# The scores of a pair of heads move from the next step into the middle of the same step's weight unit

## The chip, the cores and the metric

The kernel runs on one core of a Trainium2 chip. The metric is the time of one execution on the device in microseconds (us). Before the change it is 1480.53 us, the median of three runs (1478.89 to 1480.69).

## What is computed

Two blocks of two transformer layers each, on 256 rows of width 1024, in float32. The change touches the attention of the first block's two layers. There, eight index heads score all keys; their sum picks the 64 keys that the six heads of kind A may see. Five heads of kind B (a band with a relative bias) and five of kind C (a forgetting mask) have masks of their own. Cut to what matters:

```python
# index heads: 8 of width 64, with one common key
idx_scores = einsum('bqhs,bqh->bqs', relu(einsum('bqhd,bsd->bqhs', qis, kf)), ws)
_, sel = top_k(where(adm, idx_scores, -inf), topk)
# heads A, B, C: 16 of width 64, each with its own mask or bias
logits = einsum('bqhd,bshd->bhqs', q, k) * scale + mask
p = softmax(logits)
o = einsum('bhqs,bshd->bqhd', p, v)
# beside them, from the same normed rows h: the gates of the three branches
gates = sigmoid(h @ w_gate + b_gate)
y = (gates[0] * (o_a @ w_a) + gates[1] * (o_b @ w_b) + gates[2] * (o_c @ w_c)) @ w_out
```

## The kernel before

The 256 rows are two tiles of 128. A weight matrix comes in units of two tiles of 128 rows by 512 columns. ScalarE rounds a unit to a high part (`hi_units`, L1294), GpSimd makes the low part (`lo_units`, L730), and TensorE multiplies high by high, high by low and low by high: 12 matmuls of 512 columns a unit (L776), the first six with the unit's first tile, the last six with its second. `unit` takes a function `amid` and calls it between these two sixes.

The attention of a layer of the first block is 27 steps, k = 0 to 26, written out engine by engine in the function `attention`. The 24 heads come in pairs: four pairs of index heads (heads 0 to 7), then eight pairs of real heads (8 to 23). In its step k TensorE does in this order:

- the scores of the pair k - 1 where k is odd (`pipe["score"]` is 1): L1006 and L1009. A score contracts over 64 values, so the two heads of a pair use the upper and the lower half of the array's rows; the profile shows such matmuls as 64*128. They wait for `qk_turned` (ScalarE's copy of the turned queries and keys), for `masked` of the head before the pair (its scores have left the two banks that all pairs share, 4 and 5), and for pair 0 also for `drained` of a modulation product that used such a bank;
- the turning (transposes, L1022) of the queries and keys of the pair k, where k is even;
- the turning of the probabilities of head k - 3 (L986, `turn_head`);
- through `weave`: in steps 3 to 8 the products for a forgetting mask (L1181 to L1188), then a weight unit of the gates (steps 0 to 23) or of a branch (24 to 26). In its middle stand, where k is even and from 12 on, the products of the pair k - 4, k - 3 with V (L966, L968, `weigh_pair`). Each head takes 64 of the array's columns: 128*64 in the profile.

ScalarE in its step k rounds a weight unit, copies the turned queries and keys of the pair k (L1420 to L1425), and only then takes head k - 1: a ReLU in its bank for an index head (L1433), the exponentials for a real one (L1437, L1439). VectorE in its step k makes a forgetting mask from TensorE's products of that step (L2054, L2055, steps 4 to 8), and then takes head k - 1: for an index head it adds the bank to the sum of scores (L1870), for a real head it adds the mask (L1880, L1881); both set `masked`. Then it copies the turned probabilities of head k - 3 (L1849), on which the products with V wait, and after that come gate rows, the low part of a pair's output and a round of the search for the 64 best keys. Within an engine this order is fixed by the code. The attention of the second block (`paired` false) keeps its order.

Of the kernel before, what the change touches and what calls it, by code (L numbers as in the profile page):

```python
# [329 lines left out]
def heads_one():  # L330

    out = [dict(kind="I", h=h, q=QI + h * DH, k=KI) for h in range(HI)]
    out += [dict(kind="B", h=h, q=QB + h * DH, k=KB + h * DH, v=VB + h * DH, o=(HA + h) * DH) for h in range(HB)]
    out += [dict(kind="C", h=h, q=QC + h * DH, k=KC + h * DH, v=VC + h * DH, o=(HA + HB + h) * DH) for h in range(HC)]
    out += [dict(kind="A", h=h, q=QA + h * DH, k=KA + h * DH, v=VA + h * DH, o=h * DH) for h in range(HA)]
    return out
# [13 lines left out]
def program(nc, ctx, dram, out, cat, book):  # L350
# [101 lines left out]
    def con(name):  # L452
        a, b = cat[name]
        return CON[:, a:b]
# [30 lines left out]
    def tp_user_before(pipe, h):  # L485

        return max((g for g in range(h) if pipe["tp"][g] == pipe["tp"][h]), default=-1)

    def score_bank(pipe, h):
        return BANK[pipe["sb"][h // 2 % len(pipe["sb"])][h % 2]]  # L490
# [246 lines left out]
    def _(pe):  # L737
# [203 lines left out]
        def attention(tag, heads, src, weave, pipe, after=None):  # L941


            real = lambda h: 0 <= h < len(heads) and heads[h]["kind"] != "I"

            def weigh_head(h):
                if real(h):
                    bank = BANK[pipe["tp"][h]]
                    copied = p_turned_act if pipe["act_copies"] and h % 2 else p_turned
                    pe.wait_ge(copied.sem, copied.at((tag, h)))  # L950
                    v = heads[h]["v"]
                    pt = pipe["pt"][:, h % pipe["n_pt"], :]
                    pe.matmul(bank[:, 384:448], pt[:, 0:P], src[:, 0, v:v + DH], start=True, stop=True)  # L953
                    pe.matmul(bank[:, 448:512], pt[:, P:2 * P], src[:, 0, v:v + DH], start=True, stop=False)
                    pe.matmul(bank[:, 448:512], pt[:, 2 * P:3 * P], src[:, 1, v:v + DH], start=False, stop=True)\
                        .then_inc(headed.sem, headed.mark((tag, h)))

            def weigh_pair(h):

                if real(h) and h % 2:  # L960
                    bank = BANK[pipe["tp"][h - 1]]
                    pe.wait_ge(p_turned.sem, p_turned.at((tag, h)))
                    values = [heads[h - 1 + n]["v"] for n in range(2)]
                    turned_probs = [pipe["pt"][:, (h - 1 + n) % pipe["n_pt"], :] for n in range(2)]
                    for n in range(2):
                        pe.matmul(bank[n * DH:(n + 1) * DH, 0:S], src[:, 0, values[n]:values[n] + DH], turned_probs[n][:, 0:S], start=True, stop=False)  # L966
                    for n in range(2):
                        ins = pe.matmul(bank[n * DH:(n + 1) * DH, P:S], src[:, 1, values[n]:values[n] + DH], turned_probs[n][:, S:S + P], start=False, stop=True)  # L968
                    ins.then_inc(headed.sem, headed.mark((tag, h)))

            def turn_head(h):
                if real(h):
                    if pipe["paired"]:
                        pe.wait_ge(evened.sem, evened.at((tag, h)))
                        if h % 2 and pipe["tp"][h - 1] == pipe["tp"][h]:
                            pe.wait_ge(p_turned.sem, p_turned.at((tag, h - 1)))
                        elif real(h - 2) and pipe["tp"][h - 2] == pipe["tp"][h]:
                            pe.wait_ge(turned_lo.sem, turned_lo.at((("o", tag), (h - HI) // 2 - 1)))
                    else:
                        pe.wait_ge(exped.sem, exped.at((tag, h)))  # L980
                    if not pipe["paired"] and real(tp_user_before(pipe, h)):

                        pe.wait_ge(head_out.sem, head_out.at((tag, tp_user_before(pipe, h))))
                    bank = BANK[pipe["tp"][h]]
                    for at, cols in ((0, slice(S, S + P)), (P, slice(0, P)), (2 * P, slice(P, S))):
                        ins = pe.transpose(bank[:, at:at + P], SM[:, h % N_SM, cols], con("ident"))  # L986
                    ins.then_inc(p_in_psum.sem, p_in_psum.mark((tag, h)))

            for k in range(len(heads) + pipe["weigh"]):
                h = k - pipe["score"]  # L990
                if 0 <= h < len(heads) and h % 2 == 0:
                    pe.wait_ge(qk_turned.sem, qk_turned.at((tag, h // 2)))
                    last = h + 1 - 2 * len(pipe["sb"])
                    if last >= 0:

                        pe.wait_ge(masked.sem, masked.at((tag, last)))
                    if h == 2 and heads[0]["kind"] != "I":

                        pe.wait_ge(drained.sem, drained.at(("qkv", tag[1], -(-3 * len(heads) * DH // CW) - 1)))
                    if h == 0 and heads[0]["kind"] == "I":  # L1000
                        pe.wait_ge(drained.sem, drained.at(("ada", tag, (7, 9)[tag])))
                    slot = h // 2 % pipe["n_qk"]
                    kk = KIT[:, :] if heads[h]["kind"] == "I" else pipe["qk"][:, slot, S:2 * S]
                    for n in range(2):
                        rows_ = slice(n * DH, (n + 1) * DH)
                        pe.matmul(score_bank(pipe, h + n)[:, 0:S], pipe["qk"][rows_, slot, P:S], kk[rows_, :], start=True, stop=True)  # L1006
                    for n in range(2):
                        rows_ = slice(n * DH, (n + 1) * DH)
                        pe.matmul(score_bank(pipe, h + n)[:, S:S + P], pipe["qk"][rows_, slot, 0:P], kk[rows_, 0:P], start=True, stop=True)\  # L1009
                            .then_inc(scored.sem, scored.mark((tag, h + n)))  # L1010
                if k < len(heads) and k % 2 == 0:
                    one, two = heads[k], heads[k + 1]
                    assert one["kind"] == "I" or two["k"] - one["k"] == two["q"] - one["q"] == DH
                    if k >= 2:
                        pe.wait_ge(qk_turned.sem, qk_turned.at((tag, k // 2 - 1)))
                    with_k = one["kind"] != "I" or one["h"] == 0
                    if one["kind"] == "I" and one["h"] == 0:
                        pe.wait_ge(act_side.sem, act_side.at(("keys", tag)))
                    for what, at in (("q", 0), ("k", S))[:2 if with_k else 1]:
                        for t in range(NT):  # L1020
                            cols = KEY2[:, t, :] if one[what] == two[what] else src[:, t, one[what]:one[what] + 2 * DH]
                            ins = pe.transpose(BANK[TQ][:, at + t * P:at + (t + 1) * P], cols, con("ident"))  # L1022
                    ins.then_inc(qk_in_psum.sem, qk_in_psum.mark((tag, k // 2)))
                if pipe["paired"]:
                    turn_head(k - pipe["turn"])
                    weave(k, lambda: weigh_pair(k - pipe["weigh"]))
                else:
                    weigh_head(k - pipe["weigh"])
                    weave(k)
                    turn_head(k - pipe["turn"])  # L1030
                    if after is not None:
                        after(k)
# [95 lines left out]
        for l in range(DEPTH):  # L1128
# [29 lines left out]
            heads = heads_one()  # L1158

            def weave(k, amid, l=l):  # L1160
                if 3 <= k < 3 + HC + 1:
                    forget_products(l, k - 3)
                if k < 4 * N_GATE:
                    unit(by_key["gate", l, k // 4], k % 4, HT, amid=amid)
                else:
                    c, u = (((0, "C"), 0), ((0, "C"), 1), ((1, "C"), 0))[k - 4 * N_GATE]
                    branch_unit(l, *c, u)
                    amid()

            def branch_unit(l, cc, b, u):  # L1170

                pe.wait_ge(turned_lo.sem, turned_lo.at((("o", l), {"C": (3, 4), "B": (1, 2), "A": (N_PAIRS - 2, N_PAIRS - 1)}[b][u])))
                unit(by_key["branch", l, cc, b], u, HT if b == "A" else BT)
# [46 lines left out]
        for i in range(2):  # L1220
            heads = heads_two(i)
# [1187 lines left out]
```

## Time and profile before

| what | value |
|---|---|
| median of three runs | 1480.53 us |
| the profiled execution | 1479.98 us, its span 1478.2 us |
| TensorE busy with matmuls | 1450.4 us (98%) |
| TensorE busy with weight loads | 1214.7 us (82%) |
| VectorE, ScalarE, GpSimd busy | 720.7, 744.9, 1203.2 us |
| attention steps of layer 0 | about 121.0 to 231.0 us |
| attention steps of layer 1 | about 550.2 to 660.2 us |

The span is the time from the first to the last instruction that the profile holds; the execution is 1.8 us longer. In a timeline a row gives start, duration, engine, line, operation and tiles, and how many instructions of one kind it joins; the start plus the duration is its end. Matmuls overlap, so that a row can start before the one ahead of it has ended. In the chain of waits, the pieces lie end to end: there the cost of a group of matmuls is read directly. A float32 matmul of the scores, of V and of the transposes stands there as two records, so that L1006 x4 are two instructions.

### The profile page before, as it was taken

The page shows a single profiled execution, that of the slowest core. Times are in us where ns is not written, and L with a number is a line of the kernel's source. Part 1 is how long each engine was busy: PE and PEld are TensorE (multiplying, and loading weights), DVE is VectorE, ACT ScalarE, POOL GpSimd, SP SyncE. Part 2 cuts the span into 40 slices and gives each one's busy share as a digit, 9 for nine tenths or more (in the row PEclk, how much of TensorE's full clock was granted, in tenths as well). Part 3 has the DMA queues.
Part 4 walks back from the last instruction along what each step waited for, and adds up shares of the span by engine and source line. Part 5 has one row for each costly group of instructions (what it writes and reads, how often), then busy time and mean ns, then how long its engine had stood idle before and what let it go on. Part 6 is the DMA issues. An engine that isn't in the chain of part 4 may idle for free.

```text
span 1478.2 us, 21666 instructions
## 1 busy us (share of the span) xinstructions
PE 1450.4 (98%) x7666; PEld 1214.7 (82%) x7666; DVE 720.7 (49%) x1575; ACT 744.9 (50%) x1242; POOL 1203.2 (81%) x978
## 2 busy tenths in 40 slices
PE   7999999999999999999999999999999999999997
PEld 4898777799988988777888888778888887788886
DVE  7663664766643754745566214364650044655202
ACT  3335674644444435765544445465654345555441
POOL 4799988888878977558998989908999978489994
PEclk9999999999999999999999999999999999999999
DMA  9995547688875986337775566704555757156561
GB/s 357 387 349 177 174 161 233 223 312 312 309 264 176 394 296 215 114 98 238 236 241 186 192 199 172 239 29 157 188 193 196 221 155 226 62 163 202 192 199 57
DMA packets 149685, 313.87 MB, mean 212 GB/s; under 512 B 10933, under 2 KB 31817, under 8 KB 149577
## 3 DMA queue, kind: packets, MB, share of 16 engines
q1 hardware_dynamic: 147824, 311.15, 62.9%
q10 hardware_dynamic: 1754, 1.35, 0.3%
q8 instruction: 61, 1.00, 0.3%
q14 instruction: 46, 0.38, 0.1%
HBM read 311.39 MB, written 1.06 MB: 211 GB/s over the span
## 4 chain that ended last, share of the span: by engine, by line
PE 93%; DVE 3%; ACT 2%; POOL 1%; issue 1%; DMA 0%; SPq 0%; DVEq 0%; ACTq 0%
PE bank L776 58%; PE bank L821 12%; PE bank L822 8%; PE bank L819 5%; PE bank L1006 1%; PE bank L986 1%; PE bank L1022 1%; POOL lo_units L730 1%; PE bank L857 1%; PE bank L966 1%; DVE bank L1668 1%; ACT hi_units L1294 1%; PE bank L953 1%; PE bank L1009 1%; PE bank L1107 0%
## 5 line engine op out<-in xcount | busy, mean ns | idle before, releaser
L730 POOL TENSOR_TENSOR lo_units<-raw_units,hi_units 128x512 fp32r<-128x512 f32 (+3 forms) x928 | 1150.6, 1276 | 233.1 <-ACT hi_units L1294 232.2
L1294 ACT ACTIVATE hi_units<-raw_units 128x1024 fp32r<-128x1024 f32 (+1 forms) x470 | 483.3, 1031 | 434.4 <-PE bank L776 271.1
L776 PE MATMUL bank<-hi_units,turned 128*128 128x512 f32 (+3 forms) x1600 | 438.3, 388 | 1.5 <-DVE turned L1716 0.8
L776 PEld LDWEIGHTS bank<-hi_units,turned 128*128 128x128 f32 x1600 | 292.7, 188 | 52.7 <-issue 3.1
L822 PE MATMUL bank<-turned,lo_units 128*128 128x256 f32 x1024 | 288.2, 281 | 0.0
L776 PE MATMUL bank<-hi_units,turned_wide 128*128 128x512 f32 x992 | 274.5, 391 | 0.0
L821 PE MATMUL bank<-turned,hi_units 128*128 128x512 f32 x736 | 260.6, 399 | 0.0
L776 PE MATMUL bank<-lo_units,turned 128*128 128x512 f32 (+3 forms) x800 | 252.6, 383 | 0.8 <-POOL lo_units L730 0.5
L776 PEld LDWEIGHTS bank<-hi_units,turned_wide 128*128 128x128 f32 x992 | 185.3, 188 | 38.5 <-issue 0.5
L822 PEld LDWEIGHTS bank<-turned,lo_units 128*128 128x128 f32 x1024 | 194.3, 190 | 0.2
L776 PEld LDWEIGHTS bank<-lo_units,turned 128*128 128x128 f32 x800 | 149.8, 188 | 29.9 <-POOL lo_units L730 3.2
L821 PEld LDWEIGHTS bank<-turned,hi_units 128*128 128x128 f32 x736 | 138.3, 188 | 34.3
L776 PE MATMUL bank<-lo_units,turned_wide 128*128 128x512 f32 x496 | 160.6, 389 | 0.0
L1668 DVE SCALAR_TENSOR_TENSOR bank<-ada_units,small,bank 128x512 f32<-128x512 f32 x144 | 108.8, 756 | 36.1 <-DMA ada_units<-in_ada_w 31.5
L776 PEld LDWEIGHTS bank<-lo_units,turned_wide 128*128 128x128 f32 x496 | 93.1, 188 | 19.6
L1734 DVE TENSOR_REDUCE bank<-bank 128x256 f32<-128x512 f32 x92 | 64.3, 699 | 86.5 <-PE bank L822 85.6
L819 PE MATMUL bank<-turned,hi_units 128*128 128x256 f32 x576 | 104.0, 283 | 0.0
L819 PEld LDWEIGHTS bank<-turned,hi_units 128*128 128x128 f32 x576 | 90.2, 192 | 0.6
L1601 ACT ACTIVATE mlp_relu<-bank 128x256 f32<-128x256 f32 x56 | 21.6, 385 | 60.6 <-DVE bank L1734 60.1
L2183 DVE SCALAR_TENSOR_TENSOR bank<-x_rows,bank 128x512 f32<-128x512 f32 x8 | 5.2, 693 | 89.5 <-PE bank L776 89.5
L1730 DVE TENSOR_TENSOR turned_wide<-bank,turned_wide 128x256 fp32r<-128x256 f32 x92 | 39.0, 424 | 13.8 <-ACT turned_wide L1328 11.1
L2196 DVE SCALAR_TENSOR_TENSOR bank<-x_rows,bank 128x512 f32<-128x512 f32 x8 | 5.6, 696 | 75.4 <-PE bank L776 75.2
(264 smaller groups left out, 1325.6 us busy)
## 6 DMA issues: line engine op xcount, KB each, us to landing
ada_units<-in_ada_w SPq DMA_DIRECT2D x88, 512.0 KB, 7.8
raw_units<-in_w_ffn_tiles SPq DMA_DIRECT2D x72, 512.0 KB, 5.3
raw_units<-in_mlp_w_out SPq DMA_DIRECT2D x64, 512.0 KB, 3.3
raw_units<-in_mlp_w_tiles SPq DMA_DIRECT2D x56, 512.0 KB, 3.3
raw_units<-in_w_in SPq DMA_DIRECT2D x56, 458.0 KB, 9.8
raw_units<-in_w_in SPq DMA_DIRECT2D x48, 512.0 KB, 6.6
raw_units<-in_w_ffn_out SPq DMA_DIRECT2D x44, 512.0 KB, 3.8
raw_units<-in_moba_w_qkv SPq DMA_DIRECT2D x24, 512.0 KB, 3.8
```

Source lines behind the costliest of these rows:

```text
L730: pool.tensor_tensor(LO[:, s, b, 0:w], RAW[:, u["slot"], b, 0:w], HI_[:, s, b, 0:w].bitcast(F32), ALU.subtract).then_inc(lo_ready.sem, lo_ ...
L776: ins = pe.matmul(BANK[2 * c["pair"] + t][:, 0:w], (A[a] if A is BT else A[:, a])[:, part, t * P:(t + 1) * P], W[:, s, b, 0:w], start=(i = ...
L819: pe.matmul(bank[:, 0:S], HI_[:, s, b, at:at + P], A[:, kt, part, :], start=kt == 0 and part == 0, stop=False)
L821: pe.matmul(bank[:, :], HI_[:, s, b, at:at + P], A[:, kt, :, :].rearrange("p two s -> p (two s)"), start=kt == 0, stop=False)
L822: ins = pe.matmul(bank[:, 0:S], LO[:, s, b, at:at + P], A[:, kt, 0, :], start=False, stop=kt == KT - 1)
L857: ins = pe.transpose(BANK[(TQ, TP)[n % 2]][:, j * P:(j + 1) * P], src[:, t, (4 * half + j) * P:(4 * half + j + 1) * P], con("ident"))
L953: pe.matmul(bank[:, 384:448], pt[:, 0:P], src[:, 0, v:v + DH], start=True, stop=True)
L1294: act.activation(HI_[:, s, 0:n, 0:w], RAW[:, u["slot"], 0:n, 0:w], ACT.Copy)\
L1601: act.activation(RTN[:, m % 4, :], BANK[(TQ, TP)[m % 2]][:, 0:S], ACT.Relu).then_inc(act_side.sem, act_side.mark(("relu tile", i, m)))
L1668: ins = v.scalar_tensor_tensor(total, raw[:, k, :], COND[:, kt:kt + 1], partial, ALU.mult, ALU.add)
L1730: tell(v.tensor_tensor(AT[:, n, 1, :], h, AT[:, n, 0, :].bitcast(F32), ALU.subtract), turned_lo, (tag, "tile", n))
L1734: return v.tensor_reduce(to, bank[:, :].rearrange("p (two s) -> p s two", two=2), AX_X, ALU.add)
```

## The change

The scores become a function, `score_pair`. In the first block's layers it is no longer called at the start of step k + 1, but in the middle of step k's unit, right behind `weigh_pair`, and for the pair k that was turned at the start of this same step. The second block calls it where it stood.

```diff
-            for k in range(len(heads) + pipe["weigh"]):
-                h = k - pipe["score"]
+            def score_pair(h):
+
                 if 0 <= h < len(heads) and h % 2 == 0:
                     pe.wait_ge(qk_turned.sem, qk_turned.at((tag, h // 2)))
...
+            for k in range(len(heads) + pipe["weigh"]):
+                if not pipe["paired"]:
+                    score_pair(k - pipe["score"])
                 if k < len(heads) and k % 2 == 0:
...
                 if pipe["paired"]:
                     turn_head(k - pipe["turn"])
-                    weave(k, lambda: weigh_pair(k - pipe["weigh"]))
+
+                    def tiled(k=k):
+                        weigh_pair(k - pipe["weigh"])
+                        score_pair(k)
+
+                    weave(k, tiled)
```

No instruction is added or removed on any engine; only TensorE's order changes. Its order in steps 2 and 3 of layer 0, the pair of index heads 2 and 3 (L1022 turns its queries, L776 is the gate unit, L1006 and L1009 are its scores), before:

```order
L1022 MATMUL bank<-constants,proj_rows 128x128 [waits qk_turned]
L1022 MATMUL bank<-constants,proj_rows 128x128
L776 MATMUL bank<-hi_units,turned 128x512 [waits hi_ready]
L776 MATMUL bank<-hi_units,turned 128x512 x3
L776 MATMUL bank<-lo_units,turned 128x512 [waits lo_ready]
L776 MATMUL bank<-lo_units,turned 128x512
L776 MATMUL bank<-hi_units,turned 128x512 x4
L776 MATMUL bank<-lo_units,turned 128x512 [waits lo_ready]
L776 MATMUL bank<-lo_units,turned 128x512
L1006 MATMUL bank<-idx_keys_turned,qk_turned 128x256 [waits masked,qk_turned]
L1006 MATMUL bank<-idx_keys_turned,qk_turned 128x256
L1009 MATMUL bank<-idx_keys_turned,qk_turned 128x128 x2
```

The same place on TensorE in the changed kernel, where the turning is L1026:

```order
L1026 MATMUL bank<-constants,proj_rows 128x128 [waits qk_turned]
L1026 MATMUL bank<-constants,proj_rows 128x128
L776 MATMUL bank<-hi_units,turned 128x512 [waits hi_ready]
L776 MATMUL bank<-hi_units,turned 128x512 x3
L776 MATMUL bank<-lo_units,turned 128x512 [waits lo_ready]
L776 MATMUL bank<-lo_units,turned 128x512
L1006 MATMUL bank<-idx_keys_turned,qk_turned 128x256 [waits masked,qk_turned]
L1006 MATMUL bank<-idx_keys_turned,qk_turned 128x256
L1009 MATMUL bank<-idx_keys_turned,qk_turned 128x128 x2
L776 MATMUL bank<-hi_units,turned 128x512 x4
L776 MATMUL bank<-lo_units,turned 128x512 [waits lo_ready]
L776 MATMUL bank<-lo_units,turned 128x512
```

The scores with their two waits have moved ahead of the unit's last six matmuls; between the turning and the scores six matmuls are left of twelve.

TensorE's order in steps 12 and 13 of layer 0, from the products of heads 8 and 9 with V (L966, L968) to the turned probabilities of head 10 (L986), before:

```order
L966 MATMUL bank<-probs_turned,proj_rows 64x256 [waits p_turned]
L966 MATMUL bank<-probs_turned,proj_rows 64x256
L968 MATMUL bank<-probs_turned,proj_rows 64x128 x2
L776 MATMUL bank<-hi_units,turned 128x512 x4
L776 MATMUL bank<-lo_units,turned 128x512 [waits lo_ready]
L776 MATMUL bank<-lo_units,turned 128x512
L1006 MATMUL bank<-qk_turned 128x256 [waits masked,qk_turned]
L1006 MATMUL bank<-qk_turned 128x256
L1009 MATMUL bank<-qk_turned 128x128 x2
L986 MATMUL bank<-constants,scores 128x128 [waits turned_lo,evened]
```

The same place on TensorE in the changed kernel:

```order
L966 MATMUL bank<-probs_turned,proj_rows 64x256 [waits p_turned]
L966 MATMUL bank<-probs_turned,proj_rows 64x256
L968 MATMUL bank<-probs_turned,proj_rows 64x128 x2
L1006 MATMUL bank<-qk_turned 128x256 [waits masked,qk_turned]
L1006 MATMUL bank<-qk_turned 128x256
L1009 MATMUL bank<-qk_turned 128x128 x2
L776 MATMUL bank<-hi_units,turned 128x512 x4
L776 MATMUL bank<-lo_units,turned 128x512 [waits lo_ready]
L776 MATMUL bank<-lo_units,turned 128x512
L986 MATMUL bank<-constants,scores 128x128 [waits turned_lo,evened]
```

The products with V and the scores now stand side by side, and the six full matmuls that parted them come behind both.

## Rows read from the trace of the kernel before

**Rows 1.** The page, its first part: busy time, share and instructions of each engine.

```profile
PE 1450.4 (98%) x7666; PEld 1214.7 (82%) x7666; DVE 720.7 (49%) x1575; ACT 744.9 (50%) x1242; POOL 1203.2 (81%) x978
```

**Rows 2.** Chain of waits, layer 0, steps 8 to 14: start, duration (us), what.

```profile
157.56 2.97 PE bank L776 x12
...
168.60 1.39 PE bank L776 x6
169.99 0.58 PE bank L966 x4
170.57 0.22 PE bank L968 x4
170.79 1.58 PE bank L776 x6
172.37 0.63 PE bank L1006 x4
173.00 0.22 PE bank L1009 x4
173.22 0.48 PE bank L986 x3
...
176.90 0.33 PE bank L986 x3
```

**Rows 3.** Timeline of TensorE, layer 0: halves of the units of steps 0, 2, 4.

```profile
122.38 0.62 PE L776 MATMUL bank<-lo_units,turned 128*128 128x512 f32 x2
...
129.18 0.62 PE L776 MATMUL bank<-lo_units,turned 128*128 128x512 f32 x2
...
136.16 0.59 PE L1188 MATMUL bank<-constants,small 128*128 128x256 f32 x2
...
137.51 0.62 PE L776 MATMUL bank<-lo_units,turned 128*128 128x512 f32 x2
```

**Rows 4.** Timeline of ScalarE, layer 0, steps 0 and 2.

```profile
122.03 0.38 ACT L1422 ACTIVATE qk_turned<-bank 128x256 f32<-128x256 f32 x1
...
128.45 0.38 ACT L1422 ACTIVATE qk_turned<-bank 128x256 f32<-128x256 f32 x1 [0.25 <-PE bank L1022]
128.74 0.49 ACT L1433 ACTIVATE bank<-bank 128x384 f32<-128x384 f32 x1
```

**Rows 5.** Timeline of VectorE, layer 0, steps 0, 2 and 4.

```profile
122.17 0.69 DVE L1689 TENSOR_TENSOR mod_rows<-bank,row_vectors 128x512 f32<-128x512 f32 x1
...
129.35 0.74 DVE L1870 SCALAR_TENSOR_TENSOR idx_scores<-bank,proj_rows,idx_scores 128x256 f32<-128x256 f32 x2 [1.62 <-ACT bank L1433]
...
136.86 0.48 DVE L2054 SCALAR_TENSOR_TENSOR forget_masks<-bank,small,constants 128x256 f32<-128x256 f32 x1 [3.03 <-PE bank L1188]
...
137.64 0.74 DVE L1870 SCALAR_TENSOR_TENSOR idx_scores<-bank,proj_rows,idx_scores 128x256 f32<-128x256 f32 x2
```

**Rows 6.** Timeline of TensorE, layer 1, step 0: end of the unit's first half.

```profile
551.60 0.62 PE L776 MATMUL bank<-lo_units,turned 128*128 128x512 f32 x2
```

**Rows 7.** Timeline of ScalarE, layer 1, step 0.

```profile
551.88 1.06 ACT L1294 ACTIVATE hi_units<-raw_units 128x1024 fp32r<-128x1024 f32 x1 [0.29 <-DMA raw_units<-in_w_in]
...
553.11 0.38 ACT L1422 ACTIVATE qk_turned<-bank 128x256 f32<-128x256 f32 x1
```

**Rows 8.** Timeline of VectorE, layer 1, step 0.

```profile
552.13 0.69 DVE L1693 SCALAR_TENSOR_TENSOR mod_rows<-bank,row_vectors 128x512 f32<-128x512 f32 x1
```

**Rows 9.** Chain of waits, layer 0, step 16.

```profile
186.90 0.57 DVE probs_turned L1849
...
187.51 0.65 PE bank L966 x4
```

**Rows 10.** Timeline of TensorE, layer 0: the first halves of steps 16 and 18.

```profile
186.62 0.62 PE L776 MATMUL bank<-lo_units,turned 128*128 128x512 f32 x2
...
195.58 0.61 PE L776 MATMUL bank<-lo_units,turned 128*128 128x512 f32 x2
```

**Rows 11.** Timeline of VectorE, layer 0, step 18: the copy before the products with V.

```profile
195.42 0.56 DVE L1849 COPY probs_turned<-bank 128x384 f32<-128x384 f32 x1
```

## The prediction, made before the changed kernel was run

> **What bounds the kernel now.** I read the page first. TensorE is busy with matmuls for 1450.4 of 1478.2 us, 98%; VectorE and ScalarE stand at half of the span [rows 1]. Busy time at 98% says that TensorE rarely waits for data. It doesn't say that it works at its peak, since matmul records cover the time in which the array fills and empties. So a change of order can bring something only where the array pauses inside "busy" time, and can cost something wherever TensorE begins to wait. Next I read the chain of waits through the attention of layer 0, where the pieces lie end to end, and after that the timelines of three engines around the places to which the scores move. Layer 1 repeats layer 0 to a few hundredths, save its step 0.
>
> **What a change of the array's tiling costs now.** The chain shows four such changes for a pair of real heads. Six full matmuls of a unit, in mid-stream, take 1.39 us. L968 and L1009 are four records of 128 columns in 0.22 us; L966 and L1006 have twice the columns, so they should take 0.44 and take 0.58 and 0.63. Going from full matmuls into the products with V costs 0.58 - 0.44 = 0.14, and into the scores 0.63 - 0.44 = 0.19. Coming out: the six behind L968 take 1.58, so 0.19; the transposes behind L1009 take 0.48 where the same three behind other full matmuls take 0.33, so 0.15 [rows 2]. Twelve matmuls behind scores take 2.97, that is 2 x 1.39 + 0.19: out of the scores into a unit costs 0.19 [rows 2]. The four together: 0.14 + 0.19 + 0.19 + 0.15 = 0.67 us per pair.
>
> **What the change saves.** In steps 12, 14, 16, 18, 20 and 22 (six pairs per layer) the products with V and the scores become neighbours. What is left is 0.14 in, x between the two, 0.19 out into the unit: 0.33 + x. No row shows x, since these two never meet before. From below x is 0: both are half-array shapes, and from L966 to L968, which share a shape, nothing is paid [rows 2]. From above it is a full way out and in, 0.19 + 0.19 = 0.38. I take x = 0.19, one ordinary change, since 64*128 and 128*64 cut the array in different directions and L1006 paid 0.19 wherever it followed another shape; that is the nearest row. The saving is then 0.67 - 0.52 = 0.15 us per pair; with x = 0 it is 0.34, with x = 0.38 it is -0.04.
>
> The Trainium skill, TensorEngine Tiling (Array Packing), section Tiling Modes, Key Properties, says that changing the tiling mode drains the TensorE, while a move between tiles of one mode does not. By that rule x is not 0, since the two are separate modes in its list; by the view that only full against half counts, x would be 0. The trace agrees with the rule where it can (0.14 to 0.19 us at each change, none from L966 to L968), but has no change between the two half shapes.
>
> Two of the six can't give all of this, because TensorE is not alone at the limit there. At step 16 the first half of the unit ends at 186.62 + 0.62 = 187.24 [rows 10], VectorE's copy of the turned probabilities at 186.90 + 0.57 = 187.47, and TensorE goes on at 187.51, with L966 at 0.65 instead of 0.58 [rows 2, 9]. This gives a price for any such wait: end of what it waits for, plus 0.04 + 0.07 = 0.11, minus the end of the matmuls before. TensorE already loses 0.34 there, and if it comes earlier it waits longer: the saving of step 14 is gone. At step 18 the copy ends at 195.42 + 0.56 = 195.98, and with 0.11 at 196.09; the matmuls end at 195.58 + 0.61 = 196.19 [rows 10, 11]: room for 0.10 of the saving of step 16. Per layer: 4 x 0.15 + 0 + 0.10 = 0.70 us, for two layers 1.4 us. (x = 0: 4 x 0.34 + 0.10, twice, 2.9 us. x = 0.38: 12 x -0.04, -0.5 us.)
>
> The six other pairs (steps 0 to 10) have no products with V beside them: one way in and one way out before, the same after. I cost that at 0.
>
> **What the change adds: waits in the index heads.** The scores keep their waits, but lose as cover the six matmuls of the unit's second half (1.39 us). For the pairs 2, 4, 6 and 8 they wait until the second head of the pair before has left the bank. For pair 2 the way there is ScalarE's copy of the queries (128.45 to 128.83, it waited for L1022), then the ReLU of head 1 behind it on ScalarE, from 128.74 [rows 4], then VectorE's sum, 129.35 + 0.74 = 130.09 [rows 5]. The first half of TensorE's unit ends at 129.18 + 0.62 = 129.80 [rows 3]. Price: 130.09 + 0.11 - 129.80 = 0.40 us. That head 1 is scored earlier doesn't help: its ReLU stands behind the copy of this step's queries, and that copy needs this step's turning. For pair 4 the sum of head 3 stands on VectorE behind the forgetting mask (136.86), which waits for L1188 of the same step (136.16 + 0.59 = 136.75), and ends at 137.64 + 0.74 = 138.38 [rows 3, 5]; the half unit ends at 137.51 + 0.62 = 138.13 [rows 3]. Price: 0.36. Pairs 6 and 8 repeat this pattern, 0.36 each. Both ways start from work of TensorE in the same step, so a later TensorE doesn't shorten them. Behind the waiting scores stand the last six matmuls and everything after them; nothing later in these steps has slack to give back. Sum per layer: 0.40 + 3 x 0.36 = 1.48 us.
>
> Pair 0. In layer 0 the queries are copied by 122.03 + 0.38 = 122.41 [rows 4], and the modulation product has left its bank by 122.17 + 0.69 = 122.86 [rows 5]; with 0.11 that is 122.97, and the half unit ends at 122.38 + 0.62 = 123.00 [rows 3]: nothing. In layer 1 the half unit ends at 551.60 + 0.62 = 552.22 [rows 6], but ScalarE is behind a weight unit that waited for its DMA until 551.88, and copies the queries only at 553.11 + 0.38 = 553.49 [rows 7]. Price: 553.49 + 0.11 - 552.22 = 1.38 us. If the DMA were early, VectorE's modulation rows, 552.13 + 0.69 = 552.82 [rows 8], would still ask 0.71. I take 1.38, as the trace has it.
>
> From pair 8's successors on the wait for `masked` is free: in steps 12 to 22 VectorE does the mask before the copy for which the products with V wait anyway. ScalarE's and VectorE's own orders don't move, GpSimd and the DMA queues get no new work, and the second block is untouched: 0 for each.
>
> **Sum.** Waits 2 x 1.48 + 1.38 = 4.3 us; saving 1.4 us; net +2.9 us. The profiled execution would go from 1479.98 (span 1478.2 and 1.8 around it) to 1482.9. The median of the runs lies 0.55 above it, so I predict 1480.53 + 2.9 = 1483.4 us, slower by 0.2%. That is about what a measurement of this kernel can tell from no change (0.2%, 2.96 us), so the sign of the verdict hangs on tenths of a microsecond.
>
> **Rivals.**
> - *The two half shapes follow each other free* (x = 0). For: the two heads of a pair run beside each other without a pause in either shape. Against: every change of shape in the chain cost something. Time: waits 4.3, saving 2.9: +1.4, 1481.9 us. Chance 0.25.
> - *Clearly slower.* At the place where V and scores meet the array empties and loads in turn, x = 0.38: saving -0.5, net +4.8, 1485.3 us. For: weight loads can't be hidden across a change, and here two changes touch. Against: L966 is entered for 0.14 although it loads two halves. It decides from x = 0.20 on, where the net passes 2.96 us (4.3 - 8 x (0.34 - x) - 0.2). Chance 0.18.
> - *The index waits don't arise*, because the earlier scores pull ReLU and sum ahead in ScalarE and VectorE. For: both engines idle in these steps (1.62 us before the sum of head 1 [rows 5]). Against: the order described above. Then only pair 0 of layer 1 costs: 1.38 - 1.4, about 0, 1480.5 us; with x = 0 as well, -1.5, 1479.0 us; if that pair's DMA is early too, under 1478. Chance 0.12.
> - The forecast itself, 1483.4: 0.45.
>
> **How the numbers follow.** The forecast's own spread (the pair 0 wait from 0.7 to 1.4, x within 0.1) puts it between 1482.0 and 1484.5: of its 0.45 I put 0.26 within 0.2% and 0.19 beyond. The free change is within (0.23) or just beyond (0.02). The dear change is slower (0.17; 0.01 within). No index waits: within 0.07, faster 0.05. Faster 0.05, same 0.57, slower 0.38. Range: 1480.4, which takes in the free change and the edge of no index waits, to 1485.6, which takes in the dear change.
>
> **What would show it.** In the profile after: TensorE idle before L1006 on VectorE's L1870 (pairs 2 to 8) of 0.3 to 0.4 us, eight times, and once of about 1.3 us on ScalarE's copy in layer 1; in the chain, L966, L968, L1006, L1009 in a row, with L1006 at 0.63 for x = 0.19, 0.44 for x = 0; the step pair from one L966 to the next shorter by 0.15 except around steps 14 to 18, with the wait before L966 at step 16 growing from 0.27 to about 0.4. Wrong would be: no idle before L1006 (then the second engine orders gave way), or idle before L966 in other steps (then VectorE bounds more of the stage than I read).

## The result, and the profile after

The changed kernel takes 1483.72 us, median of 10 runs (1481.84 to 1487.38), beside 1480.08 us for the kernel before (10 runs). The ratio is 1.0023, 95% interval 1.0015 to 1.0031: slower by 2.2 to 4.6 us. The forecast was 1483.4 us, 2.9 us slower.

Who waited for whom on TensorE in the changed kernel: us in total, times, longest. These are the rows of the attention that are new or have grown:

```profile
PE bank L1006 <- DVE idx_scores L1879: 3.2, 8, 0.4
...
PE bank L966 <- DVE probs_turned L1858: 0.8, 2, 0.4
PE bank L1006 <- DVE mod_rows L1702: 0.7, 1, 0.7
```

L1006 are the scores, and L1879 is what was L1870 before (VectorE adds an index head to the sum). There are eight waits in two layers, four per layer, before the pairs 2, 4, 6 and 8. The third row is pair 0 of layer 1. L966 (products with V) waited before as well, once per layer at step 16 [rows 9]; the idle time is now 0.42 us each instead of 0.27.

The chain of waits of the changed kernel in step 2 of layer 0, where before there was no step off TensorE at all:

```profile
128.07 0.23 PE bank L1026 x2
...
128.60 0.50 ACT bank L1442
...
129.22 0.75 DVE idx_scores L1879 x2
129.97 0.14 issue
130.11 0.70 PE bank L1006 x4
130.81 0.22 PE bank L1009 x4
131.03 1.59 PE bank L776 x6
```

The way is the one of [rows 4, 5]: turning, ScalarE's ReLU behind the copy, VectorE's sum, scores. The first half of the unit had ended at 129.67 (in the timeline 129.05 + 0.62), so that without a wait L1006 would have ended at 129.67 + 0.63 = 130.30. It ends at 130.81: 0.51 us are lost. The same reckoning gives 0.45, 0.47 and 0.45 for pairs 4, 6 and 8; together 1.88 us per layer.

The chain of the changed kernel in steps 12 and 13 of layer 0, which answers to [rows 2]:

```profile
170.49 1.39 PE bank L776 x6
171.88 0.58 PE bank L966 x4
172.46 0.22 PE bank L968 x4
172.68 0.63 PE bank L1006 x4
173.31 0.22 PE bank L1009 x4
173.53 1.58 PE bank L776 x6
175.11 0.33 PE bank L986 x3
```

V and scores now stand side by side, and L1006 still takes 0.63 us: going from one half shape to the other costs 0.19, as much as coming from full matmuls. The transposes L986 have fallen from 0.48 to 0.33. From the first L966 to the next (180.37 in the same chain) it is 8.49 us; before, it was 8.61.

At step 16 of layer 0 the changed kernel waits as before, [rows 9] again:

```profile
188.67 0.57 DVE probs_turned L1858
189.24 0.04 issue
189.28 0.65 PE bank L966 x4
```

Pair 0 of layer 1 in the changed kernel, TensorE, ScalarE and VectorE, beside [rows 6 to 8]:

```profile
552.85 0.62 PE L776 MATMUL bank<-lo_units,turned 128*128 128x512 f32 x2
554.22 0.70 PE L1006 MATMUL bank<-idx_keys_turned,qk_turned 64*128 64x256 f32 x4 [0.75 <-DVE mod_rows L1702]
```

```profile
552.82 0.37 ACT L1431 ACTIVATE qk_turned<-bank 128x256 f32<-128x256 f32 x1
```

```profile
553.39 0.69 DVE L1702 SCALAR_TENSOR_TENSOR mod_rows<-bank,row_vectors 128x512 f32<-128x512 f32 x1
```

Relative to TensorE's turning, the last weight unit that ScalarE rounds before the copy, and that waits for its DMA, started 1.5 us earlier here than in the profile of before (at 551.59, with the turning at 551.48; before at 551.88, with the turning at 550.23). So its copy is done at 553.19, and VectorE's modulation rows, done at 554.09 in the chain, decide. Lost: 554.92 - (552.85 + 0.62 + 0.63) = 0.82 us.

The sum, per layer, from the turning of pair 0 to the last L966: layer 0 121.00 to 229.18 before, 120.82 to 230.50 now, +1.50 us; layer 1 550.23 to 658.39 before, 551.48 to 661.93 now, +2.29. Together 3.8 us, in the interval of the runs.

The profiled execution itself is only 2.2 us slower (1482.19 against 1479.98), since a stage whose instructions the change doesn't touch was faster in it. In the first MLP of the second block, matmuls of L821 and L822 follow each other in turns. In the ten profiles the time from one fixed turning before that stage (L857, 1021.05 in the profile of before) to the first behind it (1192.68) is either 171.6 us (the kernel before, three experiments, and a second profile of the changed kernel) or 170.3 (the first profile of the changed kernel and four experiments). The two profiles of the changed kernel alone differ by 1.38 us there. Whether the change has a hand in it is open: the four profiles in which this turning came before 1022 us all have 171.6, and of the six in which it came at 1023.8 or later five have 170.3 and one, the second of the changed kernel (1026.70), has 171.6. If the later start made the stage faster, the change would get back up to 1.4 of the 3.8 us, and that too would lie in the interval of the runs.

### The profile page after: what moved, and what is told of

Same layout as the page of the kernel before. It is cut to its first block, busy times and chain, and to the rows that moved or that the text cites. A ratio compares the mean times of both kernels' runs of the same rounds, so it can differ in the third digit from the quotient of the medians.

```text
span 1480.3 us, 21666 instructions
## 1 busy us (share of the span) xinstructions
PE 1448.0 (98%) x7666; PEld 1215.1 (82%) x7666; DVE 720.8 (49%) x1575; ACT 744.8 (50%) x1242; POOL 1203.1 (81%) x978
## 4 chain that ended last, share of the span: by engine, by line
PE 91%; DVE 4%; ACT 2%; issue 1%; POOL 1%; DMA 0%; SPq 0%; DVEq 0%; ACTq 0%
PE bank L776 57%; PE bank L821 12%; PE bank L822 8%; PE bank L819 5%; PE bank L1006 1%; PE bank L986 1%; PE bank L1026 1%; POOL lo_units L730 1%; PE bank L857 1%; PE bank L966 1%; DVE bank L1677 1%; ACT hi_units L1303 1%; PE bank L953 1%; PE bank L1009 0%; PE bank L1116 0%
## 5 line engine op out<-in xcount | busy, mean ns | idle before, releaser
L776 PE MATMUL bank<-hi_units,turned 128*128 128x512 f32 (+3 forms) x1600 | 439.6, 389 | 1.5 <-DVE turned L1725 0.8
L776 PEld LDWEIGHTS bank<-hi_units,turned 128*128 128x128 f32 x1600 | 292.0, 188 | 52.6 <-DVE turned L1782 1.2
L822 PE MATMUL bank<-turned,lo_units 128*128 128x256 f32 x1024 | 287.4, 281 | 0.0
L776 PE MATMUL bank<-hi_units,turned_wide 128*128 128x512 f32 x992 | 274.4, 391 | 0.0
L821 PE MATMUL bank<-turned,hi_units 128*128 128x512 f32 x736 | 259.2, 397 | 0.0
L776 PE MATMUL bank<-lo_units,turned 128*128 128x512 f32 (+3 forms) x800 | 252.7, 383 | 0.7 <-POOL lo_units L730 0.5
L776 PEld LDWEIGHTS bank<-hi_units,turned_wide 128*128 128x128 f32 x992 | 185.3, 188 | 38.4 <-issue 0.5
L822 PEld LDWEIGHTS bank<-turned,lo_units 128*128 128x128 f32 x1024 | 194.0, 189 | 0.2
L776 PEld LDWEIGHTS bank<-lo_units,turned 128*128 128x128 f32 x800 | 149.8, 188 | 30.1 <-POOL lo_units L730 3.2
L821 PEld LDWEIGHTS bank<-turned,hi_units 128*128 128x128 f32 x736 | 138.2, 188 | 33.6
L776 PE MATMUL bank<-lo_units,turned_wide 128*128 128x512 f32 x496 | 160.5, 389 | 0.0
L776 PEld LDWEIGHTS bank<-lo_units,turned_wide 128*128 128x128 f32 x496 | 93.1, 188 | 19.6
```

Source lines behind the costliest of these rows:

```text
L776: ins = pe.matmul(BANK[2 * c["pair"] + t][:, 0:w], (A[a] if A is BT else A[:, a])[:, part, t * P:(t + 1) * P], W[:, s, b, 0:w], start=(i = ...
L821: pe.matmul(bank[:, :], HI_[:, s, b, at:at + P], A[:, kt, :, :].rearrange("p two s -> p (two s)"), start=kt == 0, stop=False)
L822: ins = pe.matmul(bank[:, 0:S], LO[:, s, b, at:at + P], A[:, kt, 0, :], start=False, stop=kt == KT - 1)
```

## The experiments

My theory after the result: the early pairs (0 to 8) lose by waiting (1.88 us per layer, and pair 0 of layer 1), the late pairs (10 to 22) save by losing one change of shape (0.6 us per layer), and VectorE holds back part of that. The main rival: calling scores in the middle of a unit costs by itself.

### The late pairs alone

```diff
                 if not pipe["paired"]:
                     score_pair(k - pipe["score"])
+                elif (k - 1) <= HI:
+                    score_pair(k - 1)
...
                         weigh_pair(k - pipe["weigh"])
-                        score_pair(k)
+                        if not (k <= HI):
+                            score_pair(k)
```

> The change for the pairs 10 to 22 alone; the pairs 0 to 8 are scored at the start of the next step, as before. Theory (the loss is the early pairs' waits, the meeting of V and scores saves): no wait before L1006 on VectorE's index sums or on the modulation rows; L1006 right behind L968 at 0.63 us; about 0.53 us less per layer than before, 1.1 us in all, ratio 0.9993. Rival (scores in the middle of a unit cost by themselves, wherever they stand): as slow as the changed kernel or half-way, ratio 1.001 to 1.002.

Measured: 1479.66 us (11 runs) against 1479.53 for the kernel before (31 runs), ratio 1.0001 (0.9992 to 1.0009). The interval holds the expected 0.9993 and excludes the rival's 1.001 to 1.002. The profile decides more sharply: from the turning of pair 0 to the last L966 of layer 0 it is 107.66 us (before 108.18), 0.52 less, and among the waits L1006 has no row:

```profile
PE bank L986 <- ACT scores L1451: 1.8, 4, 0.7
...
PE bank L966 <- DVE probs_turned L1861: 0.8, 2, 0.4
```

So the middle of a unit costs next to nothing by itself: seven pairs per layer are scored there without a wait, and the layer is no slower. The saving stands in the trace, and is too small to tell from nothing in the times.

### The early pairs alone

The same edit with `> HI` and `not (k > HI)`.

> The change for the pairs 0 to 8 alone; the pairs 10 to 22 are scored at the start of the next step, as before. Theory: all the waits of the changed kernel and none of its saving: 2 x 1.96 us in the two layers, and 0.9 more at pair 0 of layer 1, +4.7 us on before, ratio 1.0032. Rival (the middle of a unit costs by itself): five of twelve pairs, so well under the changed kernel's ratio of 1.0023.

Measured: 1483.43 us (9 runs), ratio 1.0026 (1.0016 to 1.0036). Layer 0 takes 110.20 us from the same to the same point, +2.02. In layer 1, up to the last L966 but one, it is 104.72 against 101.95, +2.77. Together this is 4.8 us in the trace, 4.7 expected. The times show 3.9 us, with an interval of 2.4 to 5.3; this profile is one of those with the fast MLP stage. The rival is out: five of twelve pairs carry more than the whole loss.

```profile
PE bank L1006 <- DVE idx_scores L1882: 3.2, 8, 0.4
...
PE bank L1006 <- DVE mod_rows L1705: 0.7, 1, 0.7
PE bank L966 <- DVE probs_turned L1861: 0.5, 2, 0.3
```

### ScalarE and VectorE reordered

This starts from the changed kernel and touches the index head before each of the pairs 2, 4, 6 and 8. ScalarE does its ReLU ahead of the copies of the pair just turned:

```diff
                 weave(k)
+                h = k - pipe["score"]
+                early = k % 2 == 0 and 0 <= h < len(heads) and heads[h]["kind"] == "I"
+                if early:
+                    act.wait_ge(scored.sem, scored.at((tag, h)))
+                    score = score_bank(pipe, h)[:, 0:3 * P]
+                    act.activation(score, score, ACT.Relu).then_inc(exped.sem, exped.mark((tag, h)))
                 if k < len(heads) and k % 2 == 0:
...
-                if 0 <= h < len(heads) and heads[h]["kind"] == "I":
+                if early:
+                    pass
+                elif 0 <= h < len(heads) and heads[h]["kind"] == "I":
```

VectorE adds it to the sum ahead of what `weave` gives it in this step, such as the forgetting mask:

```diff
-                weave(k)
                 h = k - pipe["score"]
+                first_sum = k % 2 == 0 and 0 <= h < len(heads) and heads[h]["kind"] == "I"
+                if not first_sum:
+                    weave(k)
...
                         tell(ins, masked, (tag, h))
+                        if first_sum:
+                            weave(k)
```

> The changed kernel, and in steps 2, 4, 6 and 8 ScalarE does the ReLU of the head before the pair ahead of the copy of the pair's queries, and VectorE adds it to the sum ahead of the forgetting mask. Theory (the scores wait since these two stand behind work that needs TensorE's turning or forgetting products of the same step): the eight waits of 0.46 to 0.51 us are gone, the one at pair 0 of layer 1 stays; 3.8 us less than the changed kernel, -0.3 us on before, ratio 0.9998. Rival (ScalarE and VectorE get to head 1, 3, 5 or 7 too late in any order): the waits stay, ratio 1.0023.

Measured: 1479.71 us (11 runs), ratio 1.0001 (0.9992 to 1.0010); the expected 0.9998 lies in the interval. Step 2 of layer 0, VectorE and TensorE:

```profile
127.20 0.75 DVE L1889 SCALAR_TENSOR_TENSOR idx_scores<-bank,proj_rows,idx_scores 128x256 f32<-128x256 f32 x2 [1.77 <-ACT bank L1424]
```

```profile
127.90 0.38 PE L1026 MATMUL bank<-constants,proj_rows 128*128 128x128 f32 x2
...
129.04 0.63 PE L776 MATMUL bank<-lo_units,turned 128*128 128x512 f32 x2
129.60 0.70 PE L1006 MATMUL bank<-idx_keys_turned,qk_turned 64*128 64x256 f32 x4
```

The timeline gives L1006 0.70 us with or without a wait; the chain of this step shows that it now costs 0.63 and ends at 130.30, where it was reckoned above for no wait:

```profile
128.28 1.39 PE bank L776 x6
129.67 0.63 PE bank L1006 x4
130.30 0.22 PE bank L1009 x4
```

Head 1 is in the sum at 127.95, when TensorE has just begun to turn pair 2; in the changed kernel that was at 129.97, two microseconds later in the step. No wait on the index sums is left. So these two engines had the time; only their written order kept them. The two reorderings were made together, so this run doesn't tell their shares apart. The wait at pair 0 of layer 1 is still there (0.75 us), which is why the kernel is level with before and not ahead: layer 0 alone takes 0.34 us less than before.

### The late pairs alone, and VectorE's zeros moved

```diff
-                if k == HI + HB + ONE["score"] + 1:
+                if k == HI + HB + ONE["score"] + 4:
                     v.memset(BT[2][DH:P].bitcast(F32), 0.0)
                     link(v.memset(BT[3][0:DH].bitcast(F32), 0.0))
```

> As the kernel with the change for the pairs 10 to 22 alone, and VectorE's two clears of mixed_turned (L2073, L2074) moved from step 15 to step 18. Theory (VectorE bounds the steps 14 to 16, so that the saving of step 14 is lost there): the wait before L966 at step 16 goes, from one L966 to the next 8.49 us instead of 8.91; 0.45 us per layer less than the late pairs alone, about -2.0 us on before, ratio 0.9987. Rival (something else is late next there, ScalarE's evened probabilities or the mask): L966 waits as before, ratio 0.9993.

The edit of the late pairs alone stays in. Measured: 1477.41 us (11 runs) against 1479.53, ratio 0.9985 (0.9976 to 0.9994): the only kernel here that is clearly faster than the one before. From step 14 to 16 of layer 0, in the chain:

```profile
178.27 0.58 PE bank L966 x4
178.85 0.22 PE bank L968 x4
179.07 0.63 PE bank L1006 x4
...
184.61 0.44 PE bank L1028 x4
185.05 0.33 PE bank L986 x3
185.37 1.39 PE bank L776 x6
186.76 0.58 PE bank L966 x4
```

No VectorE stands in between, and it is 8.49 us from one L966 to the next, as expected. Layer 0 takes 107.17 us, 1.01 less than before. In layer 1 the profiled execution (1480.42 us, the slowest of the eleven) lost it again at pair 0, although that is scored at the old place:

```profile
550.66 0.38 PE L1028 MATMUL bank<-constants,idx_scores 128*128 128x128 f32 x2
555.06 0.70 PE L1006 MATMUL bank<-idx_keys_turned,qk_turned 64*128 64x256 f32 x4 [1.26 <-ACT qk_turned L1434]
```

The weights' DMA landed at 553.38, 2.7 us behind the start of this turning, and ScalarE's copy, which stands behind the rounding of these weights, ended at 555.01. What TensorE gains before this point can be lost to the DMA here; how often that happens in the timed runs isn't known.

### Pair 0 at its old place

The first edit with `(k - 1) == 0` and `not (k == 0)`, in one execution, which was profiled.

> The changed kernel with pair 0 alone scored at the start of step 1 again. Theory: the wait of L1006 for VectorE's modulation rows in layer 1 (0.75 us idle, 0.85 lost) is gone, and 0.07 in layer 0; from the turning of pair 0 to that of pair 2 6.8 us in layer 1 instead of 7.86; the eight waits on the index sums stay. Rival (ScalarE's copy is late with the weights' DMA, as in the profile of before): the copy still ends some 3 us behind the turning, and TensorE waits for it at the old place too, by up to 1.3 us.

Measured: from the turning of pair 0 (its queries) to that of pair 2 in layer 1, 551.52 to 558.56, 7.04 us, against 551.48 to 559.34, 7.86 us, in the changed kernel and 7.02 in the kernel before. The 0.82 us are back in full. (The expected 6.8 is met only if one counts from the turned keys, 0.22 us later: 6.82, where the changed kernel has 7.64.) The wait is gone, and the eight others stay at 3.2 us. One execution at 1481.39 us beside one at 1481.18 of the kernel before says nothing on the ratio. The rival didn't show here; it had in the kernel above.

### The two waits in the other order

```diff
-                    pe.wait_ge(qk_turned.sem, qk_turned.at((tag, h // 2)))
                     last = h + 1 - 2 * len(pipe["sb"])
                     if last >= 0:
                         pe.wait_ge(masked.sem, masked.at((tag, last)))
+                    pe.wait_ge(qk_turned.sem, qk_turned.at((tag, h // 2)))
```

> The changed kernel with the two waits before the scores in the other order, masked first, then qk_turned. In the changed kernel L1006 starts 0.14 us behind the end of VectorE's index sum, where L966 starts 0.04 behind that of its copy. Theory A (the later of two waits to be written is the cheap one to wait in): the 0.14 changes, to 0.04 or to more. Theory B (the 0.14 belongs to VectorE's instruction, an index sum in two of which the second releases, and not to TensorE's queue): it stays at 0.14.

Measured, in the chain of step 2 of layer 0:

```profile
128.99 0.75 DVE idx_scores L1879 x2
129.74 0.04 issue
129.78 0.70 PE bank L1006 x4
```

It is 0.04 instead of 0.14 (at all four pairs of layer 0), and the eight waits total 2.5 us instead of 3.2. Theory B is out. Of theory A it holds that the written order decides, but its direction was wrong: a wait is dear when it is written second of two, and cheap when it is written first. L1006 itself still takes 0.70. Pair 0 of layer 1 in the changed kernel agrees without any edit: when VectorE's rows, waited for second, came last, L1006 started 0.14 behind them; when ScalarE's copy, waited for first, came last (the second profile below), it started 0.04 behind it. Why, the trace doesn't show. The one execution took 1481.70 us. The Trainium skill (Perfetto Trace Analysis, Identifying Dependency Chains) notes that an instruction that waits on several engines may get separate semaphore instructions ahead of it; the two prices would fit that, but no row here shows such an instruction.

### The scores ahead of the products with V

`score_pair(k)` and `weigh_pair(...)` change places; again one execution.

> The changed kernel with the scores ahead of the products with V. Theory (every change of the array's shape costs 0.14 to 0.19 us, also between the two half shapes): L1006 0.63 behind full matmuls, L966 right behind L1009 0.58 to 0.63, the six full matmuls behind L968 1.58; from one L966 to the next 8.5 us as in the changed kernel, and 8.9 from step 14 to 16, since VectorE's work from one pair's output to the next is the same. Rival (the price belongs to the scores' and V's first load and depends on what came before): L966 at 0.44 behind the scores, 0.15 us per pair less. Second rival (the later place of the products with V gives VectorE's copy the time it lacks): no wait before L966 at step 16, 0.4 us per layer less.

Measured, in the chain of step 12 of layer 0:

```profile
171.81 0.63 PE bank L1006 x4
172.45 0.22 PE bank L1009 x4
172.67 0.58 PE bank L966 x4
173.25 0.22 PE bank L968 x4
173.47 1.58 PE bank L776 x6
```

So the price goes by what is entered: 0.19 into the scores' shape, 0.14 into V's, from full or from the other half. The sum of the three is 0.52 in either order, and the first rival (L966 at 0.44) is out. The expectation missed the steps 14 to 16: it is 9.34 us from L966 to L966 (181.09 to 190.43) against 8.9 expected, and the second rival (0.4 less) is out too. The scores now stand where the products with V stood, and wait there for VectorE's mask of the head before (L1890, once per layer, 1.5 us in all), and the products with V stand behind them, later by the scores' 0.92 us. The one execution took 1484.53 us. That VectorE's mask comes before its copy, so that the scores' wait was free behind V, is exactly what the other order gives up.

### The changed kernel once more

> The changed kernel, unaltered, for a second profile. Theory: the eight waits on the index sums and the two of L966 come back to 0.02 us, since they start from TensorE's own work; the wait at pair 0 of layer 1 is the one that moves, between 0.75 us (VectorE's modulation rows) and about 1.4 (ScalarE's copy behind a late DMA), and the pair L821, L822 in the stage from 1028 to 1107 us takes 0.347 or 0.353 us, which moves the time by 1.4. Rival: all waits repeat alike.

Measured: 1485.65 us, with the span at 1483.8 us. The eight waits are 3.2 us again and the two of L966 0.8. Pair 0 of layer 1:

```profile
554.26 0.62 PE L776 MATMUL bank<-lo_units,turned 128*128 128x512 f32 x2
556.31 0.70 PE L1006 MATMUL bank<-idx_keys_turned,qk_turned 64*128 64x256 f32 x4 [1.43 <-ACT qk_turned L1431]
```

Its start in the chain of waits:

```profile
555.98 0.28 ACT qk_turned L1431
556.26 0.04 issue
556.31 0.70 PE bank L1006 x4
```

Lost: 557.01 - (554.88 + 0.63) = 1.50 us, now to ScalarE's copy behind its DMA. The MLP stage took 171.6 us, 1.4 more than in the first profile. These two account for 2.1 of the 3.5 us between the two spans; TensorE's start (0.3 us later at the turning of pair 0 of layer 0) for another 0.3. Another 1.1 us lie between the two layers' attention, where TensorE waited twice (0.5 us) for GpSimd's low parts, which it did not in the first profile. The main rival of this run, that all waits repeat alike, is out.

Over all profiles with pair 0 in the middle of its unit, TensorE's idle time there in layer 1 is 0.7 to 0.8 us four times (the first profile of the changed kernel, the early pairs alone, the engines reordered, the scores ahead of V), and 1.2 (the waits swapped) and 1.4 us (this one), both on ScalarE's copy.

## Why the prediction was right, and where its steps were off

**The mechanism** was as told: the early pairs wait, the late pairs save one change of shape, and the first effect is larger. The two halves, each alone, show it in the trace (-0.5 us per layer for the late pairs, +4.8 us in two layers for the early ones).

**Where the index waits start** (step "what the change adds"): right for all four pairs, and the reason was tested by reordering the two engines, which removed the waits. The rival in which they don't arise is refuted for the kernel as it is, and describes the reordered one.

**Their price** was mis-sized. I took 0.11 us behind the releaser, from the one wait in the trace [rows 9]. That one waits on a single semaphore; the scores wait on two, with the late one written second, and pay 0.14 + 0.07 = 0.21. So each cost 0.45 to 0.51 us instead of 0.36 to 0.40, which makes 1.88 per layer instead of 1.48, 0.8 us in all. Swapping the waits took the extra 0.10 away.

**The price of a shape** (x = 0.19): right to the hundredth, with 0.63 for L1006 behind L968. The free change and the dear one (0.38) are both refuted. The rule of the Trainium skill (TensorEngine Tiling (Array Packing), Tiling Modes, Key Properties) that a change of tiling mode drains the TensorE agrees with the trace between the two half shapes too: 0.19 us one way, 0.14 the other.

**The saving** was put at 0.70 us per layer and is 0.58 (from the turning of pair 12 to the end of the last products with V 61.65 us, before 62.23). A full pair gives 0.12, not 0.15. From the first L966 to the next, the twelve matmuls behind the transposes take 2.77 instead of 2.76 and the next half unit 1.39 instead of 1.37, which eats 0.03 of it. That step 14 gives nothing was right (8.91 us from L966 to L966 in both), and that VectorE is the reason was shown by moving its zeros.

**The pairs without V**, put at 0 beyond their waits, cost about 0.2 us per layer, what is left of the layers' sums when waits and saving are taken off. Found are 0.07 at pair 0 of layer 0 (L1006 at 0.70), and 0.06 around pair 10, whose scores now lead into a unit (0.19) instead of into transposes (0.15); the rest is spread over hundredths.

**Pair 0 of layer 1**, put at 1.38 us, cost 0.82 in one profile of the changed kernel and 1.50 in the other. The place was right, and the floor too but for the same 0.10 (0.71 predicted if the DMA were early), but the size depends on when the DMA lands in an execution. One trace could not give it.

**The sum**: +2.9 us forecast, +3.8 in the traces' attention steps (with 0.82 at pair 0), +3.4 in the runs by their ratio. The forecast was short by 0.8 on the waits, by 0.2 on the saving and by 0.4 on the pairs without V; the early DMA of that profile took 0.6 back. That the forecast time, 1483.4 us, is within 0.4 us of the measured median (1483.72) is in part luck: had pair 0 cost the 1.38 us put down for it, the two layers would have been slower by 4.4. "Within 0.2%" was my likelier side at 0.57, and the ratio came out just beyond it, with an interval on both sides of it.

## What to carry to other kernels

Before a step is moved earlier, write down for each of its waits what the releasing engine does ahead of the release in its own written order: idle time on that engine is no help while the order stands, and becomes one when the order is changed with it. Bringing matmuls of two half-array shapes together saved one change (here 0.12 us net), while one exposed wait cost about four times that (0.45 to 0.51 us), so such a move pays only where the waits stay covered. A wait whose releaser hangs on a DMA is a range, not a number, and wants more than one profile.

## What the runs showed of the hardware that I had not expected

- Entering a shape had a price by the shape entered: 0.19 us into 64*128 (L1006), 0.14 into 128*64 (L966), from full matmuls or from the other half alike; 0.19 out into full matmuls, 0.15 out into transposes.
- With two waits written before L1006, an event waited for in the second released it after 0.14 us, in the first after 0.04. L966, with one wait, started after 0.04.
- The same stage of the same kernel ran in 171.6 or 170.3 us in different executions at a granted clock of 1.00 in both: one pair of L821 and L822 takes 0.353 or 0.347 us. What picks one of the two is open.
